# A two-block transformer kernel on one core: shared value products, alternating key and value products, and weight-panel splits in other places

## What is computed

```
q  = (rms(c_q) @ w_uq)   -> 12 heads, 64 + 32 rope
kv = (rms(c_kv) @ w_ukv) -> 12 heads: k_nope (64), v (64)
softmax(q k^T * scale, causal) @ v ; 4 more heads attend to a memory of 256 rows
```

```
kv = (h @ w_kv) -> 3 branches x (key, value) x 2 groups x 64   # 768 columns
# branch 0 is compressed: blocks of 32 tokens + cmp_pos -> @ cmp_w1 (2048 x 256) -> gelu -> @ cmp_w2
# branch 1 attends all past tokens, branch 2 a window (512: here the same), gates weigh the three
```

## Time and profile before

| | us |
|---|---|
| median of 3 runs (lowest to highest) | 3022.05 (3019.26 to 3022.43) |
| the profiled execution's own time | 3017.61 |
| its span in the trace | 3015.8 |
| PE busy | 2956.1 (98%) |
| DVE busy | 1225.8 (41%) |
| ACT busy | 1048.9 (35%) |
| DMA queue of SP, share of 16 engines | 25.4% |

### The profile page before, as it was taken

How to read it: one execution, slowest core, us unless ns; L and a number is a source line. 1 busy time by engine, 2 the same in 40 slices (tenths; PEclk the granted TensorE clock), 3 DMA queues, 4 the chain that set the end, 5 groups by cost and what they waited for, 6 DMA issues and landing times.

```text
span 3015.8 us, 36083 instructions
## 1 busy us (share of the span) xinstructions
PE 2956.1 (98%) x15464; PEld 2482.5 (82%) x15464; DVE 1225.8 (41%) x1724; ACT 1048.9 (35%) x1747; POOL 121.5 (4%) x176
## 2 busy tenths in 40 slices
PE   7999999999999999999999999999999999999998
PEld 6888888888888888888878888888888886788887
DVE  3464343343333743333664333242323358533323
ACT  3323244444443422222563222222222248532221
POOL 1000000002000100000100000010000011000000
PEclk9999999999999999999999999999999999999999
DMA  5433222223221323323303232342232330123321
GB/s 191 135 103 98 98 98 84 84 66 103 78 90 57 103 86 98 98 98 98 102 15 105 92 98 96 112 114 99 97 98 98 100 97 15 57 84 98 98 98 70
DMA packets 143807, 279.91 MB, mean 93 GB/s; under 512 B 29754, under 2 KB 42218, under 8 KB 143520
## 3 DMA queue, kind: packets, MB, share of 16 engines
q1 hardware_dynamic: 133952, 247.17, 25.4%
q0 software_dynamic: 9696, 30.44, 3.2%
HBM read 271.17 MB, written 4.25 MB: 91 GB/s over the span
## 4 chain that ended last, share of the span: by engine, by line
PE 91%; DVE 5%; ACT 2%; issue 1%; DMA 1%; SPq 0%; POOL 0%; POOLq 0%; DVEq 0%; ACTq 0%
PE bank L591 25%; PE bank L593 25%; PE bank L592 25%; PE bank L750 2%; PE bank L729 2%; PE bank L602 2%; PE bank L604 1%; PE bank L605 1%; PE bank L816 1%; PE bank L784 1%; PE bank L800 1%; PE bank L738 1%; PE bank L710 1%; DVE w_low L1682 1%; DVE xt_low L1701 1%
## 5 line engine op out<-in xcount | busy, mean ns | idle before, releaser
L1682 DVE TENSOR_TENSOR w_low<-raw,w_high 128x2048 fp32r<-128x2048 f32 (+2 forms) x212 | 479.2, 2260 | 1200.4 <-ACT w_high L1312 1194.3
L591 PE MATMUL bank<-xt_high,w_high 128*128 128x512 f32 x1984 | 779.5, 393 | 3.5 <-DVE w_low L1682 3.0
L593 PE MATMUL bank<-xt_high,w_low 128*128 128x512 f32 x1984 | 773.5, 390 | 0.0
L592 PE MATMUL bank<-xt_low,w_high 128*128 128x512 f32 x1984 | 772.7, 389 | 0.0
L1312 ACT ACTIVATE w_high<-raw 128x2048 fp32r<-128x2048 f32 (+2 forms) x212 | 400.1, 1888 | 905.1 <-PE bank L593 905.1
L591 PEld LDWEIGHTS bank<-xt_high,w_high 128*128 128x128 f32 x1984 | 372.2, 188 | 80.8 <-DVE w_low L1682 3.6
L593 PEld LDWEIGHTS bank<-xt_high,w_low 128*128 128x128 f32 x1984 | 372.0, 188 | 79.7
L592 PEld LDWEIGHTS bank<-xt_low,w_high 128*128 128x128 f32 x1984 | 372.4, 188 | 75.9
L593 PE MATMUL bank<-w_high,hidden_low 128*128 128x512 f32 x640 | 249.0, 389 | 0.0
L591 PE MATMUL bank<-w_high,hidden_high 128*128 128x512 f32 x640 | 249.0, 389 | 0.0
L592 PE MATMUL bank<-w_low,hidden_high 128*128 128x512 f32 x640 | 249.0, 389 | 0.0
(11 more groups left out here) (361 smaller groups left out, 3876.4 us busy)
## 6 DMA issues: line engine op xcount, KB each, us to landing
raw<-in_ffn_w_gu SPq DMA_DIRECT2D x80, 1024.0 KB, 5.1
raw<-in_ffn_w_down SPq DMA_DIRECT2D x44, 1024.0 KB, 5.0
raw<-in_b_w_in SPq DMA_DIRECT2D x40, 1024.0 KB, 5.2
raw<-in_a_w_in SPq DMA_DIRECT2D x24, 1024.0 KB, 5.1
raw<-in_a_w_out SPq DMA_DIRECT2D x8, 1024.0 KB, 4.9
raw<-in_ffn_w_gu SPq DMA_DIRECT2D x16, 512.0 KB, 4.4
raw<-in_w_out SPq DMA_DIRECT2D x5, 1024.0 KB, 5.0
raw<-in_w_mem_kv SPq DMA_DIRECT2D x4, 1024.0 KB, 5.2
```

The source lines that it names most:

```text
L591: pe.matmul(o, lh, rh, start=start, stop=False, skip_group_check=True)
L592: pe.matmul(o, lh, rl, start=False, stop=False, skip_group_check=True)
L593: return pe.matmul(o, ll, rh, start=False, stop=stop, skip_group_check=True)
L1682: dve.tensor_tensor(homes[n][1][:, 0:w], RAW[n % 2][:, 0:w], homes[n][0][:, 0:w].bitcast(F32), ALU.subtract).then_inc(sem["w_low_ready"], ...
```

## The change

1. **Shared keys and values.** `kv_a` now holds columns 0 to 383 and 512 to 639: the three feature products and the keys of branch 2 as a fourth. It is a plain `edge_product` with four jobs. `kv_b` holds columns 384 to 511 and 640 to 767, the values of both branches, as one token product of 256 columns. Each panel is loaded in two pieces. ACT copies each of `kv_a`'s four banks as it is done. DVE splits `kv_b`'s second panel between the two halves of the blocks.
2. **MLA.** `k_nope` and `v_rows` alternate, in other banks. The first panel of `w_out` is split where the second was (tasks 14 and 20), the second behind the attention.
3. **NSA.** The second panel of `w_out` is split behind the attention.
4. **Start.** ACT splits panel 0 ahead of row 1's square, and panel 1 behind the split of row 2; DVE splits panel 0 ahead of row 1, and panel 1 after the low parts of all rows. The low parts of rows 0 and 1 go into the wait for the inverse root of the row after.
5. **Bias rows.** DVE copies them ahead of the four bn_stats.

```diff
-    deep("kv_a", A["nsa_w_kv_2"], 0, 512)
-    deep("kv_b", A["nsa_w_kv_2"], 512, 256)
+    for k0 in (0, 4):
+        add("kv_a", [(0, 4, 512, 384, rows(wkv, k0, 4, 0, 384)), (384, 4, 512, 128, rows(wkv, k0, 4, 512, 128))])
+    for k0 in (0, 4):
+        add("kv_b", [(0, 4, 256, 128, rows(wkv, k0, 4, 384, 128)), (128, 4, 256, 128, rows(wkv, k0, 4, 640, 128))])
...
         pe.wait_ge(sem["q_roped"], at("q_roped", 1))
-        k_nope(1, 2)
+        v_rows(0, 2)
         pe.wait_ge(sem["qn_read"], at("qn_read", 3))
-        k_nope(2, 3)
+        k_nope(1, 3)
...
+        pe.wait_ge(sem["kn_read"], at("kn_read", 2))
+        v_rows(6, 5)
+        pe.wait_ge(sem["mv_read"], at("mv_read", 2))
+        v_rows(7, 6)
+        pe.wait_ge(sem["kn_read"], at("kn_read", 5))
         pe.wait_ge(sem["mv_read"], at("mv_read", 4))
...
-            edge_part(g, i, 0, jobs, None)
-            token_tiles("kv_a", i, 512, 3, 384, (0, 1))
-            turn_row("l02", 2 + i)
...
-            ins = token_tiles("kv_a", i, 512, 3, 384, (2, 3))
...
+        edge_product("kv_a", [(ps[j][:], feature(512, j * P, XTH, XTL)) for j in range(4)], "l02")
         for i, g in enumerate(ids["kv_b"]):
             pe.wait_ge(sem["w_low_ready"], at("w_low_ready", g))
-            for kk in range(4):
-                mm3(ps[4][:], *feature(256, 0, XTH, XTL)(kk, 4 * i + kk, *homes[g]), i == 0 and kk == 0, i == 1 and kk == 3)
-            ins = token_tiles("kv_b", i, 256, 5, 128, range(TT))
+            for t in range(TT):
+                operands = token(256, 0, 256, tile(t), XTH, XTL)
+                for kk in range(4):
+                    ins = mm3(ps[4 + t // 2][:, 256 * (t % 2):256 * (t % 2) + 256], *operands(kk, 4 * i + kk, *homes[g]),
+                              i == 0 and t % 2 == 0 and kk == 0, i == 1 and kk == 3)
```

ACT at the start:

```diff
-                    if t >= 2:
-                        prepare(t - 2)
+                    if t == 1:
+                        prepare(0)
                     square_rows(t, X[:, t, :], 4 * t + 2).then_inc(sem["squared_x"], step("squared_x", ("s0", t)))
+                if t == TT:
+                    prepare(1)
                 if t >= 1:
                     split_turned("s0", t - 1, XTH)
```

ACT in MLA; on DVE it is the same with n == 20:

```diff
-        prepare(ids["ukv"][0] + 1)
...
             if n == 14:
-                prepare(ids["ukv"][0] + 2)
+                prepare(ids["ukv"][0] + 1)
 
         attend_pairs("mla", next_panel)
+        prepare(ids["ukv"][0] + 2)
```

ACT for the shared keys and values:

```diff
-        after("kv_a", 0)
-        for j in range(3):
+        for j in range(4):
+            after("kv_a", j)
             act.activation(KVF[:, j, :], ps[j][:], ACT.Copy).then_inc(sem["kvf_read"], step("kvf_read", j))
```

ACT in NSA; on DVE it is the same, taken from n == 22:

```diff
-            if n == 14:
-                prepare(ids["nsa_b"][-1] + 2)
...
         attend_pairs("nsa", compressed_beside)
+        prepare(ids["nsa_b"][-1] + 2)
```

DVE at the start:

```diff
+            normed_rows("s0", 0, GB[0][:])
+            prepare(0)
+            normed_rows("s0", 1, GB[0][:], low(0))
+            normed_rows("s0", 2, GB[0][:], low(1))
+            normed_rows("s0", 3, GB[0][:])
+            low(2)()
+            low(3)()
+            prepare(1)
```

DVE in the first product (c == 0):

```diff
-            for t in range(TT):
-                dve.wait_ge(sem["v_read"], at("v_read", (c, t)))
-                link(dve.bn_stats(BN[:, 24 * t + 6 * c:24 * t + 6 * c + 6], V[:, t, 512 * c:512 * c + 512]))
             if c == 0:
                 dve.wait_ge(sem["bias_multiplied"], at("bias_multiplied"))
                 dve.tensor_copy(BROW[0:16, 0:384], ps[4][0:16, 0:384])
                 dve.tensor_copy(BROW[0:16, 384:896], ps[5][0:16, :]).then_inc(sem["bias_copied"], step("bias_copied"))
+            for t in range(TT):
+                dve.wait_ge(sem["v_read"], at("v_read", (c, t)))
+                link(dve.bn_stats(BN[:, 24 * t + 6 * c:24 * t + 6 * c + 6], V[:, t, 512 * c:512 * c + 512]))
```

DVE at the blocks of the compression:

```diff
         for j in range(2):
             dve.wait_ge(sem["kvf_read"], at("kvf_read", j))
+            if j == 1:
+                prepare(ids["kv_a"][-1] + 2)
             for g in range(2):
...
         ins.then_inc(sem["blocks_ready"], step("blocks_ready"))
-        prepare(ids["kv_a"][-1] + 2)
```

More of the change, by code:

```diff
@@ L1135, in _ @@
         pe.wait_ge(sem["q_roped"], at("q_roped", 1))
-        k_nope(1, 2)
+        v_rows(0, 2)
         pe.wait_ge(sem["qn_read"], at("qn_read", 3))
-        k_nope(2, 3)
+        k_nope(1, 3)
         pe.wait_ge(sem["q_roped"], at("q_roped", 2))
-        k_nope(3, 4)
+        v_rows(1, 4)
         pe.wait_ge(sem["qn_read"], at("qn_read", 4))
-        k_nope(4, 5)
+        k_nope(2, 5)
         pe.wait_ge(sem["qn_read"], at("qn_read", 5))
-        k_nope(5, 6)
+        v_rows(2, 6)
         pe.wait_ge(sem["k_rope_read"], at("k_rope_read", 0))
-        v_rows(0, 7)
+        k_nope(3, 7)
         pe.wait_ge(sem["k_rope_read"], at("k_rope_read", 1))
[L1148 to L1151, removed]
+        v_rows(3, 0)
+        pe.wait_ge(sem["kn_read"], at("kn_read", 0))
+        k_nope(4, 1)
+        pe.wait_ge(sem["mv_read"], at("mv_read", 0))
+        v_rows(4, 2)
+        pe.wait_ge(sem["kn_read"], at("kn_read", 1))
+        k_nope(5, 3)
+        pe.wait_ge(sem["mv_read"], at("mv_read", 1))
+        v_rows(5, 4)
+        pe.wait_ge(sem["kn_read"], at("kn_read", 2))
[3 more added lines that the diff above has]
+        pe.wait_ge(sem["kn_read"], at("kn_read", 5))
         pe.wait_ge(sem["mv_read"], at("mv_read", 4))
@@ L1591, in _ @@
             act.activation(qN[:, j, :], ps[bank][:], ACT.Copy).then_inc(sem["qn_read"], step("qn_read", j))
-        prepare(ids["ukv"][0] + 1)
-        for j in range(6):
+        for j, bank in enumerate((1, 3, 5, 7, 1, 3)):
             act.wait_ge(sem["product_done"], at("product_done", ("acc", "ukv_k", j)))
-            act.activation(kN[:, j, :], ps[1 + j][:], ACT.Copy).then_inc(sem["kn_read"], step("kn_read", j))
+            act.activation(kN[:, j, :], ps[bank][:], ACT.Copy).then_inc(sem["kn_read"], step("kn_read", j))
         def next_panel(n):
             if n == 14:
-                prepare(ids["ukv"][0] + 2)
+                prepare(ids["ukv"][0] + 1)
         attend_pairs("mla", next_panel)
+        prepare(ids["ukv"][0] + 2)
         rows("l01", ("w_out", 0))
@@ L1604, in _ @@
         rows("l02", ("down", 0, 1))
-        after("kv_a", 0)
-        for j in range(3):
+        for j in range(4):
+            after("kv_a", j)
             act.activation(KVF[:, j, :], ps[j][:], ACT.Copy).then_inc(sem["kvf_read"], step("kvf_read", j))
-        ins = act.activation(VV[:, :, 0, :], ps[3][:].rearrange("p (t n) -> p t n", t=TT), ACT.Copy)
-        ins.then_inc(sem["kvf_read"], step("kvf_read", 3))
         prepare(ids["kv_a"][-1] + 2)
         after("kv_b", 0)
-        act.activation(KVF[:, 3, :], ps[4][:], ACT.Copy)
-        act.activation(VV[:, :, 1, :], ps[5][:].rearrange("p (t n) -> p t n", t=TT), ACT.Copy).then_inc(sem["kv_copied"], step("kv_copied"))
+        for i in range(2):
+            ins = act.activation(VV[:, 2 * i:2 * i + 2, :, :].rearrange("p t b n -> p (t b n)"), ps[4 + i][:], ACT.Copy)
+        ins.then_inc(sem["kv_copied"], step("kv_copied"))
         prepare(ids["kv_b"][-1] + 2)
@@ L1721, in first_rows, with low @@
         def first_rows():
+            def low(t):
+                return lambda: low_turned("s0", t, XTH, XTL, "xt_ready")
             dve.wait_ge(sem["gains_loaded"], at("gains_loaded", "s0"))
-            for t in range(TT + 1):
-                if t < TT:
-                    if t >= 2:
-                        prepare(t - 2)
-                    normed_rows("s0", t, GB[0][:])
-                if t >= 1:
-                    low_turned("s0", t - 1, XTH, XTL, "xt_ready")
+            normed_rows("s0", 0, GB[0][:])
[6 more added lines that the diff above has]
+            prepare(1)
         def rows(s, y):
```

35 lines of the change are left out of this document (11 added, 24 removed).

## The result

The kernel after takes 2994.97 us (median of 4 runs, 2994.64 to 2995.66). Beside it the kernel before took 3020.66 (4 runs, 3018.46 to 3022.43), a ratio of 0.9914 with a 95% interval of 0.9903 to 0.9926. Forecast were 2999 us and a range of 2992 to 3006. The gain is 25.7 us (interval 22.4 to 29.3) where 23.0 were forecast.

The account below looks back on a forecast made before the run. PE was taken to bound the kernel, 91% of the chain. Keys and values -16.6, bias rows -4.4, NSA -3.2 and start +1.2 sum to -23.0 us, from 3022.05 to 2999 us; range 2992 to 3006.

Parts of the forecast that it names:

- The matmuls (9.2 us): In kv_a and kv_b, replacing 128-column matmuls with fewer of 256 columns saves 9.2 us of PE's own stream.
- Rival 3: Narrow matmuls cost by the column, so the 9.2 us saving would be 0, ending at 3008.2 us; chance 0.02.
- the stage's upper value: Top of the range for the keys-and-values gain without a cmp_w1 wait, given as 17.1 to 18.1 us.
- Two waits (4.5) and two falls (3.4): In keys and values, PE's xt_low and low-part waits go, 4.5 us, and two half-clock stretches with them, 3.4 us.
- Rival 2: The half-clock stretches do not belong to the removed waits; 5.1 us stay, ending at 3004.1 us; chance 0.11.
- cmp_w1 (0.5): After keys and values, PE newly waits for cmp_w1's second half: between 0 and 4.3 us, taken as 0.5 lost.
- Bias rows (4.4): Near 48 us, earlier bias copies remove a 2.75 us PE wait and its 1.7 us clock loss: 4.4 us gained.
- NSA (3.2): In the NSA attention, waits behind ACT's and DVE's w_out splits go: 3.2 us gained, range 2.0 to 4.0.
- MLA (0): In MLA, the moved w_out splits and alternating products change nothing: 0 us.
- The start (1.2 the other way): At the start, the first product begins 2.2 us late, an earlier full clock returns 1.0: 1.2 us lost.
- Rival 4: Late raw loads at the start make PE wait at the panels that follow, ending slower at 3027 us; chance 0.02.
- the last of the sum: The median stays 4.4 us above the profiled execution, so 3022.05 us less 23.0 us gives 2999 us.

Follow-up runs that it names:

- e6_narrow: The kernel after with each 256-column product of kv_b made as two of 128 columns; 3004.31 us.
- e1_kv: The kernel before with only the shared keys and values change (panels regrouped, copies and split reordered); 3004.09 us.
- e7_low_back: The kernel after with DVE's split of kv_b's second panel put back behind all eight block instructions; 2997.74 us.
- e11_after_again: The kernel after, unchanged, run six more times; median 2995.68 us.
- e5_no_start: The kernel after with the new order at the start undone; 2993.90 us.
- e4_start: The kernel before with only the new order at the start; 3022.29 us.
- e2_bias: The kernel before with only the bias row copies moved ahead of the four bn_stats; 3014.85 us.
- e3_nsa: The kernel before with only NSA's second w_out panel split behind the attention; 3015.96 us.
- e12_w1_split: The kernel after with the old start, DVE reordered ahead of b_w_out, and cmp_w1's second half awaited 64 matmuls later; 2990.90 us.

## Why the prediction was right, and where it was off

- **The matmuls (9.2 us).** Right. 96 token matmuls took 2002.23 to 2013.9, 0.120 apart, and `e6_narrow` measured the other side, 0.112 for the narrow ones where I had 0.110. Rival 3 is out. Two figures of the prediction do not follow from its terms: at 0.120 the saving is 9.4 us and not 9.7, and 9.4 + 4.5 + 3.4 gives 17.3 as the stage's upper value and not 18.1. Of the rule of the Trainium skill (TensorE: Matmul & The Clock Gate, "Back-to-back issue gap") the formula for isolated matmuls, about 0.056 us at 128 columns, does not hold for these, with 0.110 to 0.112, and its warning that it under-counts at small N does.
- **Two waits (4.5) and two falls (3.4).** Right: 16.9 for the stage in `e1_kv` and in after against 16.6. Rival 2 is out for these waits and for that behind the bias rows: a stretch in 12 of 12 cases with the wait, and without it no stretch of 3.4 us in these places. A wait of the same kind but of 1.33 us in `e7_low_back` had none.
- **cmp_w1 (0.5).** 0.59 in after. The load took 11.4 us to land beside SP's, 1.9 more than the same load before, without SP's beside it (9.5); the bound of 5.2 us more, one load behind the other, did not come up. That the term came out is helped by the 10.1, a median that was 0.6 above the load in question. SP's load, which the sum did not price, took 5.1 us more than its like before, and PE waited for it nowhere. Over the profiles of kernels with item 1 the wait was 0 to 1.0. That each DMA engine takes turns between the queue rows, so that loads share it, is what the Trainium skill has (DMA: Bandwidth & Descriptors, "Queues, rings and completion order"). These numbers agree: both loads became longer, and the earlier one still landed first.
- **Bias rows (4.4).** 4.34 alone, 4.6 to 4.8 with the rest.
- **NSA (3.2).** 3.47 alone and together; 0.77 of the first wait stayed, as counted, and of the second nothing. No wait at `w_out`'s later panels. The waits of 1.04 and 0.71 us ahead of it stayed, and with them the chance of a half-clock stretch (`e7_low_back`, `e11_after_again`: -1.8).
- **b_w_out (not in the sum).** +0.98 in the profile of after, -0.06 in that of `e11_after_again`: the same wait of 4.1 us with a stretch of 6.8 us or of 3.4 behind it, so not an effect of the change; the 3.4 of before is the rarer case.
- **MLA (0).** 0.05 to 0.12 in every kernel with item 2, 0.01 in those without: a cost that can be read, and no more.
- **The start (1.2 the other way).** 1.24 between `e5_no_start` and after, 1.0 in `e4_start`, each from one profile; the two profiles of the kernel after differ by 0.35 there (+1.49, +1.14). I had the first product at 20.05, and it came at 19.20, or 19.56 if x had arrived as in the trace before: 1.7 us late and not 2.2. Rival 4, loads that pace the next panels, did not come: no wait for a panel behind the start is longer than before.
- **The step that failed is the last of the sum:** "The median shown is 4.4 us above it, and nothing tells me that this part changes". It did change, and with it the median came out 4 us lower than forecast. 1.4 of the 4.4 went when the kernel before was run once more beside the other (3020.66 for 3022.05). The rest is that the profiled execution of before was an unusually good one: its 3017.61 us is below every one of 63 other times (3017.70 to 3024.72, median 3021.5), and that of after is 0.5 below the median of its ten (2995.2). The traces show part of the reason. The profile of before has 3.4 us of half clock less at b_w_out than most, worth 1.0 to 1.6 us in the table, and the profile of after had no such luck, which is its +0.98. And the wait of 2.57 us in NSA, which the change removed, let the clock fall in 2 of 4 profiles, but not in that one; `e1_kv` lost 1.0 us by it. How much of the 3.9 us between before's profile and its median each of these makes stays open.
- **The single items by their medians** gave more than by their steps too: NSA 5.1 us for 3.47 and the bias rows 6.2 for 4.34. Both steps lie inside the intervals of the ratios (1.8 to 6.9 and 2.7 to 7.9 us), so this surplus alone is not clear of noise. With 16.9 for the keys and values and 1.3 lost at the start the medians make 26.9, near the 25.7 of the whole.
- **Not foreseen at all: the long stretch.** Of the 63 times of the kernel before none is above 3024.8, and none of `e2_bias` or `e3_nsa` above 3020.5. Of the 47 times of kernels with item 1 (all but `e12_w1_split`) 7 lie 12 to 15 us above the median of their fellows, one of ten of the kernel after itself. The one that was profiled shows the stretch where item 1 put a wait in front of narrow matmuls. That item 1 brings it is shown by the counts; by which of its parts is not.

## What to carry to other kernels

Count a merge of narrow matmuls by their measured spacing, not by their columns: here half the columns cost over nine tenths of the time. Price a wait of TensorE as its length plus the clock that may fall with it, and take that second part as a chance: three waits had it every time, others in half of the executions profiled or fewer, so one profile may lack what the median has. Do not leave a wait, however short, at the head of a long run of narrow matmuls without looking at the spread of the times; and work moved from DVE to POOL must be counted twice where both run at once.

## What was not expected of the hardware

- A half-clock stretch that began in the 128 matmuls of 62 columns lasted 27.3 us and cost 13.6 us, while those behind other waits lasted 3.4 or 6.8. By the modelled ends PE was busy all through it.
- The clock fell behind NSA's waits of 1.04 and 2.57 us in some executions and not in others, with the same code.
- Of two loads that overlapped, the later and smaller one lost more: SP's 1 MB took 10.2 us for 5.1 alone, POOL's 2 MB 11.4 for 9.5.
- DVE's tensor_tensor of 128x512 took 1.66 us beside a POOL tensor_tensor, and 0.69 alone.
